# The attention stages of an encoder kernel: a ring of six in-place weight quarters, and masks added in the row maximum

## The reference

```python
for layer in range(2):
    h = rms_norm(x, norm_mix[layer])
    x = x + (mixer_ab if layer == 0 else mixer_c)(h, ...)   # layer 0: A and B heads, layer 1: C heads
    h = rms_norm(x, norm_ffn[layer])
    x = x + expert_choice_moe(h, ...)                        # 16 experts, SwiGLU, top-k by token
# inside every attention head (banded_attention)
s = einsum(q, k) * dh ** -0.5
s = where(valid, s, -1e30)          # |query - key| <= radius, inside the sequence; B heads have no mask
m = max(s, -1);  m = maximum(m, sink)  # C heads only
e = exp(s - m);  den = sum(e) (+ exp(sink - m));  o = (e / den) @ v
```

## Time and profile before

| | |
|---|---|
| median of 3 runs | 4217.72 us (4216.25 to 4220.76) |
| profiled execution | 4218.91 us, of which the instructions span 4217.1 us |
| mean granted PE clock | 0.958 of 2.4 GHz |
| busy share of the span | PE 92%, PEld 89%, DVE 63%, ACT 51%, POOL 21% |
| attention b, a, c (about) | 688, 555 and 541 us |
| the rest | output projections and experts, not touched by the change |

### The profile page before, as it was taken

The page is one execution under the profiler, slowest core; times in us unless marked ns, Lnnn a source line. Parts: engine busy times, 40 slices in busy tenths (PEclk is TensorE's granted clock), DMA queues, the critical chain, the costliest instruction groups (busy, mean ns, idle before and its releaser), DMA issues. The chain is left out here.

```text
span 4217.1 us, 75521 instructions
## 1 busy us (share of the span) xinstructions
PE 3866.0 (92%) x27368; PEld 3739.4 (89%) x27368; DVE 2650.6 (63%) x5010; ACT 2137.4 (51%) x3992; POOL 865.1 (21%) x1441
## 2 busy tenths in 40 slices
PE   7999998999978859999999969999795899999998
PEld 6988987999877759999999969999684899999998
DVE  6655654666554467777777746666425677777775
ACT  5544544556542235555556545555321555555554
POOL 5132121334420001111111123222000111111110
PEclk9999999999989979999999989999897999999999
DMA  2000001122115358877788621000343777788874
GB/s 93 19 20 10 14 9 47 52 60 68 41 46 178 117 187 255 248 240 241 250 248 250 212 84 41 29 17 17 106 140 121 226 240 242 249 249 251 249 243 130
DMA packets 486180, 584.25 MB, mean 139 GB/s; under 512 B 18128, under 2 KB 439248, under 8 KB 485968
## 3 DMA queue, kind: packets, MB, share of 16 engines
q1 hardware_dynamic: 471632, 531.18, 38.6%
q0 software_dynamic: 14336, 50.34, 5.5%
HBM read 515.25 MB, written 66.21 MB: 138 GB/s over the span
## 5 line engine op out<-in xcount | busy, mean ns | idle before, releaser
L1540 DVE TENSOR_TENSOR wl<-raw,wh 128x2048 fp32r<-128x2048 f32 x384 | 878.9, 2290 | 277.2 <-ACT wh L1495 276.7
L1495 ACT CAST wh<-raw 128x2048 fp32r<-128x2048 f32 x384 | 732.2, 1907 | 25.0 <-DMA raw<-in_w_gate 22.8
L1636 PE MATMUL ps_g<-xT,wh 128*128 128x384 f32 x2048 | 598.6, 358 | 3.2 <-DVE xT L1546 3.2
L1636 PE MATMUL ps_u<-xT,wh 128*128 128x384 f32 x2048 | 594.8, 357 | 0.0
L151 PE MATMUL psP<-wh,hTh 128*128 128x384 f32 (+1 forms) x1344 | 466.7, 347 | 30.1 <-DVE wl L774 24.3
L1638 PE MATMUL ps_g<-xT,wl 128*128 128x192 f32 x2048 | 478.6, 254 | 0.0
L1638 PE MATMUL ps_u<-xT,wl 128*128 128x192 f32 x2048 | 477.0, 253 | 0.0
L153 PE MATMUL psP<-wh,hTl 128*128 128x384 f32 (+1 forms) x1344 | 447.1, 333 | 0.0
L152 PE MATMUL psP<-wl,hTh 128*128 128x384 f32 (+1 forms) x1344 | 446.9, 332 | 0.0
L1018 PEld LDWEIGHTS psO<-V,pT 128*128 128x128 f32 x3456 | 421.1, 193 | 16.9 <-issue 9.1
L1018 PE MATMUL psO<-V,pT 128*128 128x64 f32 x3456 | 417.6, 273 | 1.7 <-ACT pT L714 1.2
(11 more groups left out here) (204 smaller groups left out, 8724.0 us busy)
## 6 DMA issues: line engine op xcount, KB each, us to landing
raw<-in_w_gate SPq DMA_DIRECT2D x128, 1024.0 KB, 5.4
raw<-in_w_up SPq DMA_DIRECT2D x128, 1024.0 KB, 5.3
raw<-in_w_down SPq DMA_DIRECT2D x128, 1024.0 KB, 8.3
xb<-in_x SPq DMA_DIRECT2D x72, 256.0 KB, 2.8
out_y<-yb SPq DMA_DIRECT2D x24, 512.0 KB, 5.1
h_rows<-hb SPq DMA_DIRECT2D x24, 512.0 KB, 3.5
wraw<-in_w_a SPq DMA_DIRECT2D x22, 384.0 KB, 3.3
xb<-in_x SPq DMA_DIRECT2D x12, 512.0 KB, 4.2
```

What stands on the lines that cost most here:

```text
L1495: act.copy(wh[:, j % SPL], raw[:, j % RAW]).then_inc(w_high, 1)
L1540: dve.tensor_tensor(wl[:, j % SPL], raw[:, j % RAW], wh[:, j % SPL].bitcast(F32), ALU.subtract)\
L1636: both = lambda **fl: pe.matmul(ps[:, f, 0:2 * CAP], wh[:, j % SPL, k, fs], xT[:, k].rearrange("p h c -> p (h c)"), **fl)
```

## The change

In every attention phase:

1. `wh`, `wl` and the raw quarters have six slots (RING = 6). The raw quarter lies in the same bytes as `wl` of its slot: DVE reads raw and `wh` and overwrites raw with `wl`. A quarter is loaded when PE has finished the half projection that read the slot (`projected` now counts halves), and no longer when a raw buffer is free.
2. W events move. In a and c, quarters 0 and 1 of the next turn are converted after tiles 5 and 7, and quarters 2 and 3 between the two halves of the next turn's first tile. In b, the conversion in the middle of the tiles is gone: 0 and 1 follow the first two of the remaining units, 2 and 3 lie between the halves as in a and c.
3. At the start of a phase ACT's first conversion waits for its gain (`gn_in`) and its quarter, no longer for all constants. Loads of x in a no longer wait for the weights' conversion.
4. The mask matmul is gone. DVE's `tensor_reduce` over both heads of a unit becomes one `tensor_tensor_reduce` for each head, which adds the mask to the scores, writes them back to PSUM and takes the maximum. In b, without masks, `tensor_reduce` stays.

```diff
-RING, RAWQ, LAG, HELD = 5, 2, 5, 4
+RING, LAG, HELD = 6, 5, 4
+LEAST = -3.0e38
...
             got.append(("P", p, half))
+            if p and p % NT == 0 and half == 0:
+                got += [("W", p // NT * WQ + 2), ("W", p // NT * WQ + 3)]
...
-                if t == 5 and i + 1 < self.N:
-                    events.append(("W", (i + 1) * WQ))
-                if t == NT - 1 and i + 1 < self.N:
-                    events.append(("W", (i + 1) * WQ + 1))
+                if t in (5, 7) and i + 1 < self.N:
+                    events.append(("W", (i + 1) * WQ + (t - 5) // 2))
...
-            if 0 <= p < self.total - 1 and p % NT == NT - 1:
-                events += [("W", (p // NT + 1) * WQ + q) for q in (2, 3)]
...
+    low_at = -(-nc.sbuf_base // 32) * 32
     wl = ph.sb("wl", [P, RING, KW, NC], F32R)
+    raw = nc.alloc_sbuf_tensor_at(f"raw_{state['n']}", [P, RING, KW, NC], F32, offset=low_at)
...
-                sp.wait_ge(w_split, q % RAWQ + 1 if q < WQ + RAWQ else q - RAWQ + 1)
-                sp.dma_start(wraw[:, q % RAWQ], weights(q)).then_inc(w_in[q % RAWQ], 16)
+                if q >= RING:
+
+                    i, quarter = divmod(q - RING, WQ)
+                    sp.wait_ge(projected, 2 * (i * NT + NT - 1) + quarter // 2 + 1)
+                sp.dma_start(raw_quarter(q), weights(q)).then_inc(w_in[q % RING], 16)
...
                     if e[1] == 0:
-                        act.wait_ge(const_in, 16 * NCONST)
+                        act.wait_ge(gn_in, 16)
                     weight_high(e[1])
...
-                chain.link(dve.tensor_reduce(nmax[:, r, hs], psS[:, u % 2, :].rearrange("p (c k) -> p c k", c=ns)[:, :, 0:w],
-                                             AX.X, ALU.max, negate=True))
+                if masks is None:
+                    ins = dve.tensor_reduce(nmax[:, r, hs], psS[:, u % 2, :].rearrange("p (c k) -> p c k", c=ns)[:, :, 0:w],
+                                            AX.X, ALU.max)
+                else:
+                    at = segs[0][4] - mask0
+                    for c in range(ns):
+                        ps = psS[:, u % 2, c * 512:c * 512 + w]
+                        ins = dve.tensor_tensor_reduce(ps, ps, maskf[:, at:at + w], 1.0, LEAST, ALU.add, ALU.max,
+                                                       nmax[:, r, off + c:off + c + 1])
+                chain.link(ins)
...
-                if half == 1:
-                    ins.then_inc(projected, 1)
+                ins.then_inc(projected, 1)
...
-                        ins = pe.matmul(out, q, kT[:, kv, 1, ks], start=False, stop=mask is None)
-                        if mask is not None:
-                            at = mask - mask0
-                            ins = pe.matmul(out, identr[:, :], maskr[:, at:at + w], start=False, stop=True)
+                        ins = pe.matmul(out, q, kT[:, kv, 1, ks], start=False, stop=True)
```

More of the change, by code:

```diff
@@ L327, in dense_order @@
                 plan.append(unit)
-                if x < WQ - 1 and not last:
-                    plan.append(("W", (i + 1) * WQ + 1 + x))
+                if x < 2 and not last:
+                    plan.append(("W", (i + 1) * WQ + x))
         events = [("N", 0, 0), ("N", 0, 1), ("W", 0), ("W", 1), ("N", 1, 0), ("N", 1, 1), ("W", 2), ("W", 3)]
@@ L477, in attention_phase @@
     psO = ph.psum("psO", [P, 512])
[L480 to L490, removed]
+    const_in, ident_in, gn_in = ph.sem("const_in"), ph.sem("ident_in"), ph.sem("gn_in")
+    w_in = [ph.sem(f"w_in{x}") for x in range(RING)]
     x_in = [ph.sem(f"x_in{x}") for x in range(XH)]
@@ L503, in attention_phase @@
     half_ready, tally = ph.sem("half_ready"), ph.sem("tally")
-    NCONST = 2 + NS + (masks is not None) + (sink is not None)
+    NCONST = 1 + NS + (masks is not None) + (sink is not None)
     def place(p):
@@ L514, in raw_quarter @@
     def raw_quarter(q):
-        return first_w[q] if q < WQ else wraw[:, q % RAWQ]
+        return raw[:, q % RING]
     def tile_cols(p):
@@ L549, in load_w @@
                     return
[L551 to L555 removed]
+                if q >= RING:
+                    i, quarter = divmod(q - RING, WQ)
+                    sp.wait_ge(projected, 2 * (i * NT + NT - 1) + quarter // 2 + 1)
+                sp.dma_start(raw_quarter(q), weights(q)).then_inc(w_in[q % RING], 16)
+            sp.dma_start(ident, identity).then_inc(ident_in, 16)
+            if work.norms[0][0] == 0:
                 load_x(0)
                 load_x(1)
[L558 to L566 removed]
+            sp.dma_start(gn[:, :], norm_gain).then_inc(gn_in, 16)
+            load_w(0)
+            load_w(1)
+            for x in range(2 if work.norms[0][0] == 0 else 0, XH):
+                load_x(x)
+            load_w(2)
+            load_w(3)
             for s, st in enumerate(steps):
                 sp.dma_start(gains[:, s, :], st["gain"]).then_inc(const_in, 16)
+            sp.dma_start(rope[:, :, :, :, :], table).then_inc(const_in, 16)
+            if masks is not None:
+                sp.dma_start(maskf[:, :], masks).then_inc(const_in, 16)
             if sink is not None:
@@ L571, in _ @@
             ph.clear_previous(sp)
-            if work.norms[0][0] != 0:
-                for x in range(XH):
-                    load_x(x)
+            load_w(4)
+            load_w(5)
             for e in events:
@@ L577, in _ @@
                     load_x(2 * e[1] + e[2] + XH)
-                if e[0] == "W" and e[1] >= RAWQ:
-                    load_w(e[1] + RAWQ)
+                if e[0] == "P" and e[1] % NT == NT - 1:
+                    for quarter in (0, 1):
+                        load_w(e[1] // NT * WQ + RING + 2 * e[2] + quarter)
                 if e[0] == "V":
@@ L638, in weight_high @@
             def weight_high(q):
[L639 to L645 removed]
+                act.wait_ge(w_in[q % RING], 16 * (q // RING) + 16)
                 for k in range(KW):
@@ L667, in evacuate @@
                     act.wait_ge(rt_ready, n[-1] + 1)
-                act.wait_ge(projected, p + 1)
+                act.wait_ge(projected, 2 * p + 2)
                 act.copy(xr[:, b, :], psP[:, 0:nh * HD])
@@ L908, in _ @@
                 if e[0] == "P" and e[2] == 1:
+                    if e[1] == 0:
+                        constants()
                     tile_up_to(3)
```

49 lines of the change are left out of this document (10 added, 39 removed).

## The result

| | before | after |
|---|---|---|
| median | 4216.99 us (4 runs, 4212.57 to 4220.76) | 4152.92 us (4 runs, 4150.38 to 4159.12) |
| ratio | | 0.9851, 95% interval 0.9834 to 0.9868 |
| span of the profiled execution | 4217.1 us | 4149.5 us |

The change makes the kernel 1.5% faster: 64 us in the medians, 67.6 in the profiled spans. The windows of the changed kernel, cut at the same marks as the earlier trace rows: stages b, a and c, an ordinary tile of c from its first R to the next, the turn change of the earlier trace rows, and the tile behind it. A row gives the stretch, its length, the busy us (and instructions) of PE, PEld, DVE, ACT and POOL, the mean PE clock, the DMA share and GB/s.

What follows compares the result with a forecast made beforehand. PE's time and waits were taken as the bound. Masks 41, starts 16.8, turn changes 3.6 (c) and 10 (a), and stage b 2 sum to 73.4 us: 4218.9 - 73 = 4145 us, range for 8 in 10 4105 to 4180.

Steps and rivals of the forecast that it cites:

- Masks: All mask matmuls of a and c: 48.2 us if PE is the bound, less 7, so 41 us gained.
- quarters 0 and 1 are converted in cover: At turn changes of a and c: converting the next turn's quarters 0 and 1 was given no cost.
- the 7 us for tiles with x: Taken off the mask gain: five tiles of c's first turn lose 0.7 us each, plus the last five tiles of a and c.
- Starts: Starts of stages b, a and c: ACT's first conversion no longer waits for constants; 16.8 us gained, bounds 8 and 21.
- of the 6.67 I take 5.8: Start of b: of ACT's 6.67 us wait for constants, 5.8 us counted as gained.
- quarters 2 and 3 still land before PE has done the first half: Start of a: quarters 2 and 3, now behind 512 KB of x, still land before PE finishes the first half projection.
- Turn changes of a: Five changes in a: new waits of 14 us in sum for 24.0 now; 10 us gained.
- the clock's loss as now: Turn changes of a and c: PE's low clock after the gap was taken to cost as much as before.
- the turn changes vanish: Rival: ACT runs further ahead or the clock does not fall, new waits and clock loss unpaid; about 4115 us, chance 0.12.
- Turn changes of c: Three changes in c: PE waits 3.8 us at a new place; 1.2 us gained each, 3.6 us with the short waits gone.
- Half speed of the masked maximum: Rival: the new DVE maximum runs at half throughput, costing 0.7 us in each of c's 48 tiles; 4180 us, chance 0.13.
- the slower rival: The new maximum has a high fixed price; at 1.29 us each the masks bring nothing; about 4265 us at 1.7, chance 0.04.

Runs made afterwards that it cites:

- mask half alone: The kernel before with only the masked maximum in place of the mask matmul; ring, conversions and starts as before: 4187.43 us, ratio 0.9923.
- cover run: The changed kernel with quarters 0 and 1 of the next turn converted between the halves of tiles 5 and 7 of a and c: 4137.50 us, ratio 0.9813.
- ahead of T: The changed kernel with quarters 2 and 3 at turn changes of a and c converted behind the step's scores, not between the halves: 4127.36 us, ratio 0.9784.
- the maximum twice: The changed kernel with every masked maximum done twice in a row: 4239.44 us, ratio 1.0054 to the kernel before.
- constants awaited: The changed kernel with a stage's first conversion waiting again for all constants, not only its gain: 4170.30 us, ratio 0.9894.
- x first: The changed kernel, at starts of b and c, with two x squares ahead of the first conversion and quarters 4 and 5 loaded later: 4148.90 us, ratio 0.9832.
- the ring alone: The changed kernel with mask matmul and tensor_reduce as before the change; six slots, moved conversions and starts kept: 4175.27 us, ratio 0.9906.

## Why the prediction was right, and which of its terms were not

Forecast 4145, measured 4152.9: the direction, the places and most of the mechanisms were right. Three terms were off, each by about as much as the whole sum or more: ordinary tiles 9 us under the forecast, the starts 6 under, the turn changes of a 11 over. That these nearly cancel is luck. (The bounds given for the likeliest case add up to 4123 to 4170, not 4120 to 4165.)

- **Masks: 41 us forecast.** The mask half alone brings 31.1 in its profile, or about 34 without the low clock in b. The price a matmul was right (0.69 to 0.74 us for a tile of c of 384 columns, 0.24 for one of a), and the unit's 1.25 us was 1.12. What failed in the change is "quarters 0 and 1 are converted in cover": they cost 12.9 us of the ordinary tiles, read off the cover run (24 us gained there in the change, 37 with that edit, 33 forecast). And the 7 us for tiles with x left out the 3 us of a's turns 1 and 3.
- **Starts: 16.8 forecast, about 10 measured** (b 2.2, a 4.0, c about 4), near the lower bound of 8. ACT's first conversion started at 7.74 in b and 3.4 us behind the first quarter's issue in a, as forecast. The step that failed in b is "of the 6.67 I take 5.8": the conversion came 5.4 us earlier and PE's first projection only 1.5. PE waits there for the fifth half tile of x, whose load waits for the first square (the kind of wait that I did see in c) and then takes 7 us to land. In c the first projection comes 2.0 us earlier, counted from the first issue of its weights, for 3.6 forecast. In a, "quarters 2 and 3 still land before PE has done the first half" was wrong: ACT waited 3.85 us for them and PE 2.0. But how much that costs is chance: six other profiles with the same order of loads have waits of PE of 0.7 to 1.5 us there, and gained 7.0 to 8.0 us at the start of a, near the 7.4 forecast, where the change's profile gained 4.0. Part of this is the clock. The second tile of a in the change, then in "ahead of T":

```profile
703.21:710.10 6.89, 6.48 (x27) 6.21 (x28) 1.58 (x6) 1.06 (x4) 2.55 (x5) 0.73 0.00 0
701.04:706.23 5.19, 4.79 (x27) 4.52 (x27) 1.58 (x6) 1.06 (x4) 2.56 (x5) 1.00 0.01 5
```

- **Turn changes of a: 10 forecast, about 21 without the masks' share.** The waits came out as said (2.2 to 2.7 us, in sum 12.2 for 14). The step that failed is "the clock's loss as now". Windows of the changes' first tiles, two of before, two of after:

```profile
789.84:800.35 10.51, 10.51 (x58) 10.47 (x56) 5.49 (x18) 3.58 (x11) 2.26 (x5) 0.74 0.15 44
1077.71:1086.68 8.97, 8.97 (x51) 8.87 (x50) 4.78 (x15) 4.97 (x14) 1.86 (x5) 0.75 0.14 46
```

```profile
774.78:785.13 10.35, 7.89 (x56) 7.47 (x55) 7.31 (x23) 5.58 (x15) 2.91 (x6) 1.00 0.16 60
1047.12:1056.33 9.21, 6.96 (x50) 6.72 (x49) 6.58 (x21) 7.15 (x20) 3.20 (x7) 1.00 0.31 114
```

  A mean of 0.74 over 10.51 us costs 10.51 x 0.26 = 2.7 us. Behind the shorter waits three of the five have 1.00. By the same sum over the three tiles around each change, an estimate, the clock cost 13.7 us before and 3.4 after: 10 of the 11 us that the term was short. That is the rival "the turn changes vanish" in part.
- **Turn changes of c: 3.6 forecast (8 with the masks' share), 5.8 measured.** The wait was 3.4 for 3.8, and the clock was worse in one of them than in the two others, behind the same wait.
- **Stage b: 2 forecast, 3.9 measured**, the two quarters between the halves cost nothing.
- **Half speed of the masked maximum** is out: 580 ns at 384 columns. The break-even of the slower rival was too high. By its formula, with 6.89 - 1.91 us of other work on DVE between the same marks, the kernel with the maximum twice has y = (9.57 - 4.98) / 4 = 1.15 us, under the break-even of 1.29, and it was already slower than before. I had priced only c's ordinary tiles, by DVE's idle time, and a's and c's tiles with x and the turn changes at nothing.

## What to carry to other kernels

Work put "into cover" costs what stands behind it in its engine's queue: look at the instructions behind the place, not at the busy share of the tile. The best of the places tried for a conversion is where its engine waits for the busy one, here between the halves of a projection (15 us), or ahead of work that is wanted later (26 us). When the bounding engine gets shorter work ahead of a fixed chain, part of the gain becomes a wait at that chain: two halves of a change that meet at one place don't add up.

## What the runs showed that I had not expected

The clock behind a wait of the same length is not the same. In the first tile of a turn of c, with a wait of 3.38 or 3.39 us for `wl`, four kernels (the change, cover, constants awaited, x first) give 12 windows: their mean clock is 1.00 twice, 0.89 seven times, and 0.79, 0.72 and 0.65 once each. By length, the tile is 13.51 us at 1.00 and 19.60 at 0.65. With a wait of 2.71 us (the ring alone) or 1.38 (quarters ahead of T) it was 1.00 in three of three each. A short wait alone doesn't decide it: in a, waits of 2.0 to 2.7 us at the five changes of these four kernels and the ring alone left the clock at 1.00 in 11 of 25 windows, and at 0.66 to 0.86 in the others. So a microsecond less of such a wait in c can be worth 1.4 to 6 more, and one execution's profile says little on which. Of the kernel with all constants awaited, and of that with x first:

```profile
2684.47:2697.98 13.51, 10.13 (x75) 9.77 (x73) 9.46 (x30) 7.29 (x20) 2.81 (x5) 1.00 0.04 12
```

```profile
2670.17:2689.77 19.60, 16.21 (x74) 15.79 (x73) 10.10 (x32) 7.80 (x22) 2.81 (x5) 0.65 0.03 8
```
